# Layer norm sums taken tile by tile in the projection, statistics on 128x4 numbers, spread back by a product with a diagonal

## The reference, cut to what matters

```python
def _layernorm(x, g, b):
    mu = xf.mean(-1, keepdims=True)
    var = jnp.square(xf - mu).mean(-1, keepdims=True)
    y = (xf - mu) * lax.rsqrt(var + LN_EPS) * g + b
...
x = _layernorm(DEEPNORM_ALPHA * x + (1 + gt1) * y, ln_g[i, 0], ln_b[i, 0])
hin = x * (1 + sc2) + sh2
y = _swiglu(hin, ffn_w_in[i], ffn_w_out[i])
x = _layernorm(DEEPNORM_ALPHA * x + (1 + gt2) * y, ln_g[i, 1], ln_b[i, 1])
```

## Time and profile before

| | us |
|---|---|
| median of 3 runs | 3007.53 (3005.47 to 3011.3) |
| the profiled execution | 3009.08 |
| its span, first to last instruction | 3007.2 |
| PE busy | 2776.0 (92% of the span) |
| DVE busy | 1364.7 (45%) |
| ACT busy | 1032.5 (34%) |
| POOL busy | 224.3 (7%) |

### The profile page before, as it was taken

One profiled execution on the slowest core, in us unless ns is written; L12 is line 12 of the kernel. 1 busy time (PEld: TensorE's weight loads), 2 busy tenths in 40 slices (PEclk: granted clock), 3 DMA queues, 4 the chain that ended last, 5 costly groups with the idle time before them and its releaser, 6 DMA issues.

```text
span 3007.2 us, 46336 instructions
## 1 busy us (share of the span) xinstructions
PE 2776.0 (92%) x18854; PEld 1991.9 (66%) x18854; DVE 1364.7 (45%) x2209; ACT 1032.5 (34%) x1560; POOL 224.3 (7%) x204
## 2 busy tenths in 40 slices
PE   4999998889999799989999699999899897899998
PEld 1566666368888445658888488887465565788875
DVE  7565565243332266653333443334224766433335
ACT  1334342153421224544431344321111573444214
POOL 1232332010000103210000000000000100000000
PEclk9999999899999899999999899999979999999999
DMA  5334433322232011022232122222021002222212
GB/s 214 107 124 131 142 124 101 112 70 98 98 110 86 33 63 36 29 78 93 95 114 96 42 84 95 93 110 98 28 85 56 16 2 70 84 98 98 100 71 88
DMA packets 46996, 260.83 MB, mean 87 GB/s; under 512 B 5080, under 2 KB 7528, under 8 KB 28040
## 3 DMA queue, kind: packets, MB, share of 16 engines
q1 hardware_dynamic: 46280, 254.23, 24.5%
q10 hardware_dynamic: 576, 4.57, 0.4%
HBM read 256.63 MB, written 2.15 MB: 86 GB/s over the span
## 4 chain that ended last, share of the span: by engine, by line
PE 86%; DVE 5%; ACT 3%; DMA 1%; POOL 1%; issue 1%; PEld 1%; SPq 0%; DVEq 0%; ACTq 0%; PEldq 0%; POOLq 0%
PE psum L213 85%; PE psum L1686 2%; DMA weights<-in_ada 1%; PEld psum L213 1%; POOL ysum L543 0%; DVE ln_rstd L1249 0%; POOL branch_in L545 0%; DVE weights L249 0%; DVE rms_rstd L1329 0%; ACT L589 0%; POOL join L538 0%; DVE ff_weights_lo L1361 0%; DVE ffn_weights_lo L1361 0%; DVE keys_rstd L2295 0%; ACT yg L623 0%
## 5 line engine op out<-in xcount | busy, mean ns | idle before, releaser
L1361 DVE TENSOR_TENSOR ff_weights_lo<-weights,ff_weights_hi 128x1024 fp32r<-128x1024 f32 (+1 forms) x120 | 159.7, 1332 | 329.3 <-ACT ff_weights_hi L1358 329.3
L1361 DVE TENSOR_TENSOR ffn_weights_lo<-weights,ffn_weights_hi 128x1024 fp32r<-128x1024 f32 (+1 forms) x120 | 159.7, 1332 | 322.3 <-ACT ffn_weights_hi L1358 322.2
L213 PE MATMUL psum<-ff_in_hi,ff_weights_hi 128*128 128x512 f32 x704 | 276.3, 392 | 21.0 <-DVE ff_in_lo L1258 17.6
L213 PE MATMUL psum<-ffn_in_hi,ffn_weights_hi 128*128 128x512 f32 x704 | 276.1, 392 | 17.9 <-DVE ffn_in_lo L1337 14.4
L1358 ACT ACTIVATE ffn_weights_hi<-weights 128x1024 fp32r<-128x1024 f32 (+1 forms) x120 | 137.4, 1147 | 448.2 <-PE psum L213 448.2
L1358 ACT ACTIVATE ff_weights_hi<-weights 128x1024 fp32r<-128x1024 f32 (+1 forms) x120 | 137.4, 1146 | 445.3 <-PE psum L213 445.3
L213 PE MATMUL psum<-ffn_in_lo,ffn_weights_hi 128*128 128x512 f32 x704 | 275.6, 391 | 0.0
L213 PE MATMUL psum<-ff_in_lo,ff_weights_hi 128*128 128x512 f32 x704 | 275.6, 391 | 0.0
L213 PE MATMUL psum<-ff_in_hi,ff_weights_lo 128*128 128x512 f32 x704 | 275.3, 391 | 0.0
L213 PE MATMUL psum<-ffn_in_hi,ffn_weights_lo 128*128 128x512 f32 x704 | 275.2, 391 | 0.0
L213 PEld LDWEIGHTS psum<-ff_in_hi,ff_weights_hi 128*128 128x128 f32 x704 | 133.2, 189 | 50.9 <-issue 19.2
(11 more groups left out here) (458 smaller groups left out, 4940.1 us busy)
## 6 DMA issues: line engine op xcount, KB each, us to landing
weights<-in_ada SPq DMA_DIRECT2D x96, 512.0 KB, 4.2
weights<-in_ff_in SPq DMA_DIRECT2D x44, 1024.0 KB, 4.8
weights<-in_ffn_in SPq DMA_DIRECT2D x44, 1024.0 KB, 4.8
weights<-in_ff_out SPq DMA_DIRECT2D x16, 1408.0 KB, 5.8
weights<-in_ffn_out SPq DMA_DIRECT2D x16, 1408.0 KB, 5.8
weights<-in_rwkv SPq DMA_DIRECT2D x8, 1152.0 KB, 5.7
weights<-in_fox_qkv SPq DMA_DIRECT2D x4, 1536.0 KB, 6.5
weights<-in_rwkv SPq DMA_DIRECT2D x8, 640.0 KB, 4.0
```

The lines of the kernel that those rows point to most:

```text
L213: return nc.tensor.matmul(out, lhsT, rhs, start=start, stop=stop)
L1361: return nc.vector.tensor_tensor(sp_.lo[u][:, 0:width], slot[s][:, u * width:(u + 1) * width], sp_.hi[u][:, 0:width].bitcast(F32), ALU.sub ...
```

## The change

While a projection runs, ACT squares each finished tile of `x` and DVE adds the squares up (`Sums`), in all seven projections; where a layer norm follows, DVE also adds up the tiles themselves. Both totals cover tiles 0 to 6. In the last tile of the projection PE sums the total of squares: ahead of its second half in a split projection, two blocks before the end in `project`. Where an RMS norm follows this is one product with ones; where a layer norm follows, it is four products in which the 128x128 block of the total is the stationary operand and one column of ones moves, which leaves the sums by tokens, 128 tokens by 4 columns. The last tile is added in the norm, from `x` and from its square.

The layer norm works out mean, variance, root and reciprocal on 128x4 numbers. DVE multiplies the identity by the reciprocals (a diagonal matrix for each of the four groups of tokens), and a product with ones spreads them over all partitions in PSUM. The mean is also made over all partitions by two products with ones, and DVE subtracts it tile by tile, just ahead of the scaling, reading both from PSUM. The root's table is touched ahead of the last square. The low parts of the first weight tile move from DVE to GpSimd in the layer norms, and the alpha steps wait until the last tile has gone through. The loops over tiles become straight code. `rms1` and the norms inside the attention keep their way.

The diff, cut: the removed lines of `total_of` and its neighbours, of the loops and of `split_project` stand in the functions above; `split_project`'s DVE program changes as its ACT program does.

```diff
+        square, squares_total = keep("tile_squares", [P, 2, T]), keep("squares_total", [P, T])[:, :]
...
-        def total_of(factor):
...
+        class Sums:
+
+            def __init__(self, name, mean):
+                self.mean = mean
+                self.dve = steps_again("sums_mean_dve" if mean else "sums_dve", [
+                    n for j in range(KT) for n in [f"squares{j - 1}"] * (j >= 2) + [f"sum{j}"] + [f"total{j}"] * (mean and 1 <= j < KT - 1)])
+                self.act = steps_again("sums_act", [f"square{j}" for j in range(KT)])
+                self.last = self.dve, f"sum{KT - 1}"
+
+            def square(self, act, j):
+
+                act.wait_ge(*self.dve(f"sum{j}"))
+                nc.scalar.activation(square[:, j % 2, :], x[:, j, :], ACT.Square).then_inc(*self.act.step(f"square{j}"))
+
+            def update(self, dve, j, product, factor):
+
+                if j >= 2:
+                    if j >= 3:
+                        dve.wait_ge(*self.dve(f"squares{j - 2}"))
+                    dve.wait_ge(*self.act(f"square{j - 1}"))
+                    nc.vector.tensor_tensor(squares_total, square[:, 0, :] if j == 2 else squares_total, square[:, (j - 1) % 2, :],
+                                            ALU.add).then_inc(*self.dve.step(f"squares{j - 1}"))
+                dve.wait_ge(*product)
+                f = factor if isinstance(factor, float) else mod(*factor, j)
+                nc.vector.scalar_tensor_tensor(x[:, j, :], ps[:, j % 2, :], f, x[:, j, :], ALU.mult, ALU.add).then_inc(
+                    *self.dve.step(f"sum{j}"))
+                if self.mean and 1 <= j < KT - 1:
+                    if j >= 2:
+                        dve.wait_ge(*self.dve(f"total{j - 1}"))
+                    dve.wait_ge(*self.dve(f"sum{j}"))
+                    nc.vector.tensor_tensor(tiles_total, x[:, 0, :] if j == 1 else tiles_total, x[:, j, :], ALU.add).then_inc(
+                        *self.dve.step(f"total{j}"))
+
+            def first_tiles(self, pe):
+
+                pe.wait_ge(*self.dve(f"squares{KT - 2}"))
+                if not self.mean:
+                    mm(ps[:, 5, :], ones, squares_total, True, False)
+                    return
+                for q in range(QT):
+                    mm(ps[:, 7, q:q + 1], squares_total[:, q * P:(q + 1) * P], ones[:, 0:1], q == 0, False)
...
-                with pe.Fori(0, n) as i:
...
+                for j in range(KT):
+                    i, s = j // 2, j % 2
+                    pe.wait_ge(*loads[s].arrived(i))
+                    if j >= 2:
+                        pe.wait_ge(*sums.dve(f"sum{j - 2}"))
+                    for k, src in enumerate(sources):
+                        if j == KT - 1 and k == len(sources) - 2:
+                            sums.first_tiles(pe)
+                        last = mm(ps[:, s, :], wtile(s, k), src, k == 0, k == len(sources) - 1)
+                    last.then_inc(*pe_done.step(f"product{s}"))
+
+            def act(act):
+                sums.act.enter(act)
+                for j in range(KT - 1):
+                    sums.square(act, j)
...
-            mean, std, rstd = (keep(f"{name}_{n}", [P, T], scope) for n in ("mean", "std", "rstd"))
-            sq = keep(f"{name}_sq", [P, 2, T], scope)
+            spread = keep(f"{name}_spread", [P, QT, P], scope)
+            st = keep(f"{name}_stat", [P, 5, QT], scope)
+            MEAN, LESS, VAR, STD, RSTD = range(5)
...
-                pe.wait_ge(*reached(*ready[KT]))
-                mm(ps[:, 4, :], ones, tiles_total).then_inc(*pe_done.step("sum"))
-                for j in range(KT):
-                    pe.wait_ge(*act_done(f"sq{j}"))
-                    mm(ps[:, 5, :], ones, sq[:, j % 2, :], j == 0, j == KT - 1).then_inc(*pe_done.step(f"sq{j}"))
+                for q in range(QT):
+                    mm(ps[:, 6, q:q + 1], tiles_total[:, q * P:(q + 1) * P], ones[:, 0:1], q == 0, False)
+                pe.wait_ge(*sums.dve(f"sum{KT - 1}"))
+                for q in range(QT):
+                    last = mm(ps[:, 6, q:q + 1], x[:, KT - 1, q * P:(q + 1) * P], ones[:, 0:1], False, q == QT - 1)
+                last.then_inc(*pe_done.step("sums"))
+                pe.wait_ge(*sums.act(f"square{KT - 1}"))
+                for q in range(QT):
+                    last = mm(ps[:, 7, q:q + 1], square[:, (KT - 1) % 2, q * P:(q + 1) * P], ones[:, 0:1], False, q == QT - 1)
+                last.then_inc(*pe_done.step("squares"))
+                mm(ps[:, 4, :], ones, tiles_total, True, False)
+                mm(ps[:, 4, :], ones, x[:, KT - 1, :], False, True).then_inc(*pe_done.step("mean"))
+                pe.wait_ge(*dve_done("spread"))
+                mm(ps[:, 5, :], ones, spread[:, :, :].rearrange("p q n -> p (q n)")).then_inc(*pe_done.step("rstd"))
 
             def act(act):
                 act_done.enter(act)
-                act.wait_ge(*pe_done("sum"))
-                nc.scalar.activation(mean[:, :], ps[:, 4, :], ACT.Copy, scale=1.0 / D).then_inc(*act_done.step("mean"))
-
-                nc.scalar.activation(std[:, 0:1], const("ln_eps"), ACT.Sqrt).then_inc(*act_done.step("table"))
-                for j in range(KT):
-                    act.wait_ge(*dve_done(f"centred{j}"))
-                    if j >= 2:
-                        act.wait_ge(*pe_done(f"sq{j - 2}"))
-                    nc.scalar.activation(sq[:, j % 2, :], x[:, j, :], ACT.Square).then_inc(*act_done.step(f"sq{j}"))
+                act.wait_ge(*sums.dve(f"squares{KT - 2}"))
+                nc.scalar.activation(square[:, KT % 2, 0:1], const("ln_eps"), ACT.Sqrt).then_inc(*act_done.step("table"))
+                sums.square(act, KT - 1)
                 if units:
-                    units.first(act, units.first_hi)
-                act.wait_ge(*pe_done(f"sq{KT - 1}"))
-                act.wait_ge(*act_done("table"))
-                nc.scalar.activation(std[:, :], ps[:, 5, :], ACT.Sqrt, bias=const("ln_eps"), scale=1.0 / D).then_inc(*act_done.step("std"))
+                    units.first_hi(act, 0)
+                act.wait_ge(*dve_done("least"))
+                nc.scalar.activation(st[:, STD, :], st[:, VAR, :], ACT.Sqrt, bias=const("ln_eps")).then_inc(*act_done.step("std"))
+                if units:
+                    units.first_hi(act, 1)
...
+                small, fused = nc.vector.tensor_scalar, nc.vector.scalar_tensor_tensor
+                dve.wait_ge(*pe_done("sums"))
+                small(st[:, MEAN, :], ps[:, 6, 0:QT], 1.0 / D, None, ALU.mult).then_inc(*dve_done.step("mean"))
+                dve.wait_ge(*dve_done("mean"))
+                fused(st[:, LESS, :], st[:, MEAN, :], -1.0, st[:, MEAN, :], ALU.mult, ALU.mult).then_inc(*dve_done.step("less"))
                 if following:
                     l, sh, sc, to = following
-                    dve.wait_ge(*reached(*ready[KT - 1]))
                     a, b = l * 48 + sh * KT, l * 48 + sc * KT
                     nc.vector.tensor_tensor(shift[:, :], vec[:, VC["ln_b"][0] + col:VC["ln_b"][0] + col + KT], mods[:, b:b + KT],
                                             ALU.mult).then_inc(*dve_done.step("b scale"))
                     dve.wait_ge(*dve_done("b scale"))
                     nc.vector.tensor_tensor(shift[:, :], shift[:, :], mods[:, a:a + KT], ALU.add).then_inc(*dve_done.step("shift"))
-                dve.wait_ge(*act_done("mean"))
-                for j in range(KT):
-                    nc.vector.tensor_tensor(x[:, j, :], x[:, j, :], mean[:, :], ALU.subtract).then_inc(*dve_done.step(f"centred{j}"))
-                if units:
-                    units.first(dve, units.first_lo)
+                dve.wait_ge(*pe_done("squares"))
+                dve.wait_ge(*dve_done("less"))
+                fused(st[:, VAR, :], ps[:, 7, 0:QT], 1.0 / D, st[:, LESS, :], ALU.mult, ALU.add).then_inc(*dve_done.step("var"))
+                dve.wait_ge(*dve_done("var"))
+                small(st[:, VAR, :], st[:, VAR, :], 0.0, None, ALU.max).then_inc(*dve_done.step("least"))
                 dve.wait_ge(*act_done("std"))
-                nc.vector.reciprocal(rstd[:, :], std[:, :]).then_inc(*dve_done.step("rstd"))
+                nc.vector.reciprocal(st[:, RSTD, :], st[:, STD, :]).then_inc(*dve_done.step("rstd"))
                 dve.wait_ge(*dve_done("rstd"))
-                for j in range(KT + 2):
+                nc.vector.tensor_tensor(spread[:, :, :], ident.unsqueeze(1).to_broadcast([P, QT, P]),
+                                        st[:, RSTD, :].unsqueeze(2).to_broadcast([P, QT, P]), ALU.mult).then_inc(*dve_done.step("spread"))
+
+                def centred(j):
+                    fused(x[:, j, :], ps[:, 4, :], -1.0 / D, x[:, j, :], ALU.mult, ALU.add).then_inc(*dve_done.step(f"centred{j}"))
+                dve.wait_ge(*pe_done("mean"))
+                centred(0)
+                for j in range(KT + 1):
                     if j < KT:
```

(72 more changed lines are left out.)

128 lines of the change are left out of this document (24 added, 104 removed).

## The result

The changed kernel takes 2973.07 us (median of four runs, 2969.55 to 2979.42), the kernel before on the same chip 3008.19 (3005.47 to 3011.3). The ratio is 0.9885, with a 95% interval of 0.9866 to 0.9905: faster by 1.15%. The forecast was 2980.0 with a range of 2969 to 2995. Five more runs of the changed kernel in a later session gave 2967.24 to 2983.53; the median of all nine is 2972.2. They spread over 16 us; those of the kernel before spread over 6 in the first session and 7 in the later one.

The account below looks back on a forecast made before the run. TensorE is 86% of the chain, so only its waits or work can give time. -37.2 (layer norms) + 4.4 + 1.6 + 2.8 + 0.9 = -27.5: 3009.08 becomes 2981.6, median 2980.0; range 2969 to 2995, own range 2973 to 2989.

Parts of the forecast that it names:

- rival 1: Layer-norm tails: the clock stays full until R in all four, R = 6.2; total 2972 us; chance 14%.
- The sums early: Layer norms: totals of tiles 0 to 6 ready early shorten the tails, within 37.2 us gained over four stretches.
- R = 8.0, from 6.2 to 8.9: Layer-norm tail: us from the last product's end to the diagonal product's end; 6.2 at full clock, 8.9 if it falls early.
- about 4 us in: Layer-norm tail: PE's clock falls to half about 4 us after the last product, one mean product fast, the rest slow.
- rival 2: Stream after the tail: PE runs at half clock throughout, 2.56 us for six products; total 3004 us, no change; chance 9%.
- The stream, 2.08 us a tile: After R: VectorE's scaled, centred and low part pace each tile at 2.08 us; lo7 at R + 16.9, half tile R + 17.9.
- GpSimd's splits cost nothing: ln00, ln10: first two weight splits on GpSimd, 2.5 to 3.5 us each, end before PE wants them at 11.6.
- Alpha steps beside the next split, +0.3: ln00, ln10: GpSimd's eight alpha steps now run after lo7, beside the next weight split, adding 0.3 us.
- Thin products in the last product, 1.1 each: Last product ahead of each layer norm: four one-column products on PE add 1.1 us, 4.4 us in all.
- The stalls, 1.6 and 1.4: Last products of dsa_out and mix_out: PE waits for the sum of squares, 1.6 and 1.4 us.
- rms2 nothing, mix_out and rms3 2.8, rms4 0.9: RMS norms: rms2 saves 0.89 and pays 0.87; mix_out with rms3 costs 2.8 us; rms4 pays 0.87.
- Rival 4: Projections: straight code brings PE's instructions late; gain gone at 0.49 us a tile, 3019 us at 0.7; chance 4%.

Follow-up runs that it names:

- experiment 3: Changed kernel with layer-norm statistics back on 128x512 numbers (no diagonal, thin products or clamp), sums still early: median 2976.38 us, ratio 0.9885.
- experiment 5: Against the changed kernel with PSUM statistics, full-width product first, squares' product later: tiles 1 to 7 not centred, 2954.27 us; or three unused full-width products added, 2966.01 us.

## Why the forecast was right, and where it was off

The direction and the main mechanism were right, and the size fell short by 7 us in the median, 12 in the profiled execution. The median stands at the edge of the forecast's own range of 2973 to 2989, and nearer to rival 1's 2972 than to 2980. That is in part luck: rival 1's cause, a full clock until R in all four, did not come true. By its own steps:

- **The sums early.** Right, and the main part: with the statistics on full-width numbers about 41 of the 45 us remained (experiment 3). The split's move to GpSimd, 2.36 us of the chain of before in each of two norms, is among them.
- **R = 8.0, from 6.2 to 8.9.** Mis-sized: 7.4, 6.9, 7.7 and 5.7 us, worth 4.3 us in all (to the first scaled tile; to the end of the product with the diagonal, as the forecast had it, 0.1 less each). Two errors stood against each other. Four thin products took 0.95 us and not 1.1, so that R at full clock was 5.7, below the lower bound; and the clamp held for 1.65 us in two norms lay in nobody's sum. The fall of the clock "about 4 us in" came between 1.1 and 9.4 us in the profiled tails. Rival 1 (full clock until R) was true of ln00 and ln11; rival 2 (half clock all through) was true of no stream.
- **The stream, 2.08 us a tile.** Mis-sized: neighbours overlap by more than was taken, 1.86 us a tile (starts 0.66, 0.60 and 0.60 apart). lo7 ended at R + 15.5 for 16.9, the half tile at R + 16.6 for 17.9; the pairs of ln01 and ln11 took 1.39 for 1.45. Worth 3.5 us in all. With R's 4.3 this accounts for 44.7 us against the 37.2 of the forecast. That VectorE paces it was right (experiment 5).
- **GpSimd's splits cost nothing.** The splits took 2.34 us (forecast 2.5 to 3.5), ended 8.5 us after the last product, and no product waited for them. But the cost was not nothing: 1.65 us in each of two norms on VectorE. The step looked at when the split ends, and not at what it meets on the way. The prediction's rule, "by it only spread is slowed", asked only for two SBUF inputs, and so missed `least`, which has one. The Trainium skill, "SBUF — State Buffer", section "SBUF: two separate sides", has the wider rule: a VectorE operation that reads two inputs from SBUF, or that runs in a mode which uses two ports, shares a pair of ports with GpSimd under an exclusive lock, and whoever starts first keeps it for the whole instruction. The traces agree. The small held operations ended 0.02 to 0.03 us after GpSimd's; the reciprocals, with one SBUF input, were not held; and the spread held GpSimd's second split (2.80 us for 2.35). Whether the clamp ran in a mode with two ports no run here shows.
- **Alpha steps beside the next split, +0.3.** Right in kind: that split took 1.73 us in ff0 and 1.58 in ff1, where it takes 1.23 elsewhere, so 0.5 and 0.35.
- **Thin products in the last product, 1.1 each.** 0.9 each.
- **The stalls, 1.6 and 1.4.** 1.54 and 1.49: right.
- **rms2 nothing, mix_out and rms3 2.8, rms4 0.9.** 0.9 won, 3.6 lost, 0.9 lost. Rms2 gained 0.9 since its sum with ones ran at full clock (1.14 us for 2.05).
- **What no step had.** 3.3 us behind ln01, where the half clock lasted 6.8 us in place of 13.6, and 1.6 lost at the start of ff1's loop, which began at half clock. Both are the clock's state at a moment, not work that the change touched.
- **Rival 4, late instructions of straight code.** Not seen: "issue" is 1% as before.

## What to carry to other kernels

Add a norm's sums up while the product runs: that is where most of the time was, several times what the small arithmetic behind it gave (about 4 of 45 us). Before work goes to GpSimd, list what VectorE starts while it runs, and give those operations that read two inputs from SBUF, and small clamps like `least`, an operand in PSUM, or start GpSimd behind them. Where a tail hangs on TensorE, read the granted clock in several executions before one of them is trusted, and don't crowd one-column products around its start: a tail of 5.7 us at full clock took up to 8.9.
